# Long-convolution filters on both halves of TensorE's array, with the norm's magnitudes added on GpSimd

## The chip, the cores and the metric

The kernel runs on one core of one Trainium2 chip. The metric is the device time of one execution in microseconds (us), the median of several runs. All line numbers are those of the kernel before the change.

## What is computed

A backbone of two layers over 512 latent tokens and 256 context tokens of width 1024. Each layer has attention, a short convolution and a long ("Hyena") convolution in parallel, and then a mixture of 16384 experts of which 16 are picked for each token and head. The part that the change touches makes the filters of the long convolution:

```python
z = jnp.concatenate([t, jnp.cos(bands * w), -jnp.sin(bands * w)], axis=-1)
h = jnp.sin(f1 * (z @ w1 + b1))
h = jnp.sin(f2 * (h @ w2 + b2))                      # (L, 64)
h = (h @ w3).reshape(L, HY_ORDER, 2, HY_W)           # 2 orders, 2 directions, 512 channels
h = h * jnp.exp(-t[:, :, None] * jnp.abs(decay))[:, :, None, :]
h = h / jnp.sum(jnp.abs(h), axis=(0, 2), keepdims=True)
hf, hb = h[:, :, 0], h[:, :, 1]
k = jnp.concatenate([hf, jnp.zeros_like(hf[:1]), hb[:0:-1]], axis=0)
return jnp.fft.rfft(k, axis=0)
```

L is 512 for the latents (both layers) and 256 for the context (first layer alone). The sum of magnitudes runs over all L times and both directions, for each order and channel.

## The kernel before

The program is a row of phases with a barrier between them. In a phase each engine has a list of instructions of its own, in the order in which the code issues them, and they meet at semaphores. Nothing is planned at run time: what stands behind a wait on an engine's list waits too.

**Hidden rows.** `FilterMlp` (L689) makes the 64 hidden rows of the filter's network. TensorE multiplies (L717), VectorE adds the bias and scales (L726), GpSimd reduces the angle in nine steps (L741 to L754) and ScalarE takes the sine (L760); then the same again for the second layer of the network. In layer 1 this runs inside `phase_mod`, which streams 24 blocks of modulation weights: ScalarE rounds block n (L827), VectorE makes its low part (`split`, L264), TensorE multiplies (L872), and a row copy `keep` (L821) follows every second block. The first sine stands behind block 12, the second behind block 23 and ahead of the last `keep`; the filter's matmuls on TensorE stand behind blocks 2 and 13, VectorE's part behind 3 and 14. VectorE ends the stage with six normalisations (L910) and the modulation step (L912, L917), TensorE turns it (L884), ScalarE copies it out (L845) and SyncE stores it (L800). In layer 2 the same lies in `phase_mod_beside`, beside the expert gathers.

**Filters, layer 1.** `phase_spectrum` (L1898) runs four times: latents order 0 and 1, context order 0 and 1, each ahead of its long convolution. For each tile t of 128 times (nt = 4 for latents, 2 for the context) TensorE multiplies the 64 hidden rows by the two direction blocks of w3 (L1941), in the upper 64 rows of the array, VectorE multiplies by the window (L1983; the window is ScalarE's exponential, L1970), ScalarE takes the absolute value (L1975), and TensorE sums it over the times by a matmul with ones, two per tile, accumulated in bank 4 (L1931, `norm`). Then VectorE folds the two directions (L1996, L1998), tile 0 last, after a row that needs the norm (L1991). TensorE's spectrum jobs (L1960), nine of four tiles for latents and five of two for the context, take the tiles in the order 1, 2, ..., 0 and use the cosine and sine tables.

**Filters, layer 2.** `phase_spectrum_beside` (L2025) runs twice and does the same while the last experts of layer 1 are worked off: gathers by GpSimd (L490), dots by VectorE (L650), weights by ScalarE (L503, L507, L514), sums by TensorE (L535). `Share` gives each engine a part of these after each tile or job; 50 gathers fall on the 13 steps of one such phase. GpSimd issues gathers up to three past a step's share (`FETCH`) into a ring of 8 buffers, and a gather waits until TensorE has used the buffer. The norm matmuls there are L2073, the filter's L2081, absolute value L2120, window multiply L2150, folds L2137 to L2143, jobs L2102. `filter_weights` (L2018) lists the loads of the next filter's weights.

The two f32 passes of a matmul are two instructions in the profile.

Of the kernel before, what the change touches and what calls it, by code (L numbers as in the profile page):

```python
# [27 lines left out]
P = 128  # L28
# [11 lines left out]
W_BR = 512  # L40
# [648 lines left out]
class FilterMlp:  # L689
# [67 lines left out]
    def scalar(self, act, i, hidden):  # L757
        act.wait_ge(self.reduced, i + 1)
        out = hidden if i else self.h1
        self.c.nc.scalar.activation(out[0:FH, 0:self.width], self.r[0:FH], ACT.Sin).then_inc(self.sined, 1)  # L760


def phase_mod(c, layer, lay):
# [19 lines left out]
    with Phase(nc) as ph:  # L783
# [32 lines left out]
        def _(act):  # L816
# [6 lines left out]
            for n in range(2 * chunks):  # L823
                act.wait_ge(w_landed[n % RAW], 16 * (n // RAW + 1))
                if n >= DEEP:
                    act.wait_ge(halves_done, n - DEEP + 1)
                nc.scalar.activation(hi[n % DEEP], raw[:, n % RAW], ACT.Copy).then_inc(hi_ready, 1)  # L827
                if n >= 3 and n % 2:
                    keep((n - 3) // 2)
                if SQUARES <= n < SQUARES + NT:  # L830
                    t = n - SQUARES
                    if layer == 0 and t == 0:
                        act.wait_ge(x_in, 64)
                    if t >= 2:
                        act.wait_ge(sq, t - 1)
                    nc.scalar.activation(junk[:, t % 2], c.xs[:, t], ACT.Square,
                                         accum_out=c.stat[:, 0, t:t + 1]).then_inc(sq, 1)
                if n == SQUARES + NT + 1:
                    act.wait_ge(ms, 1)
                    nc.scalar.activation(c.stat[:, 1, 0:NT], c.stat[:, 1, 0:NT], ACT.Sqrt).then_inc(root, 1)  # L840
                if n in (12, 23):
                    mlp.scalar(act, n // 23, lay.hidden)
# [3 lines left out]
                                 ACT.Copy).then_inc(rows_made, 1)  # L846

# [7 lines left out]
        def _(pe):  # L855
# [9 lines left out]
            for n in range(2 * chunks):  # L865
# [11 lines left out]
                if n in (2, 13):  # L877
                    mlp.tensor(pe, n // 13)
# [8 lines left out]
        def _(dve):  # L887
# [7 lines left out]
            for n in range(2 * chunks):  # L895
# [4 lines left out]
                if n in (3, 14):  # L900
                    mlp.vector(dve, n // 14)
# [996 lines left out]
def phase_spectrum(c, layer, length, order, lay):  # L1898
# [7 lines left out]
    w3, absdec = c.at(152, 2 * W_BR), c.at(190, W_BR)  # L1906
# [6 lines left out]
    with Phase(nc) as ph:  # L1913
# [3 lines left out]

        @ph.block.sync
        def _(sp):
            sp.dma_start(w3[0:FH, :], io["hy_w3"][layer][:, order * 2 * W_BR:(order + 1) * 2 * W_BR]).then_inc(w3_in, 16)  # L1920
# [6 lines left out]
        def _(pe):  # L1927
            def norm(t):
                pe.wait_ge(ab_d, t + 1)
                for d in range(2):  # L1930
                    last = nc.tensor.matmul(c.bank(4), c.ones[:], ab[t % 2][:, d * W_BR:(d + 1) * W_BR],  # L1931
                                            start=(t == 0 and d == 0), stop=(t == nt - 1 and d == 1))
                last.then_inc(normed, 1)

            c.warm_up(ph, pe, 7)
            pe.wait_ge(w3_in, 16)
            for t in range(nt):
                if t >= 2:
                    pe.wait_ge(hw_d, t - 1)
                for d in range(2):  # L1940
# [22 lines left out]

        @ph.block.scalar
        def _(act):
# [12 lines left out]
        def _(dve):  # L1978
# [7 lines left out]
            for t in t_order:  # L1986
                if t == 0:
                    dve.wait_ge(normed, nt)
# [29 lines left out]
def filter_weights(c, layer, order):  # L2018

    io = c.io  # L2020
    return [(c.at(126, 2 * W_BR)[0:FH, :], io["hy_w3"][layer][:, order * 2 * W_BR:(order + 1) * 2 * W_BR]),
            (c.at(130, W_BR), io["hy_decay"][layer][order:order + 1].to_broadcast([P, W_BR]))]


def phase_spectrum_beside(c, layer, order, lay, share, keep):  # L2025
# [5 lines left out]
    w3, absdec, win, hw = c.at(126, 2 * W_BR), c.at(130, W_BR), c.at(80, nt, W_BR), c.at(136, nt, 2 * W_BR)  # L2031
    ab, rnorm, bias, kre_b = [c.at(at, 2 * W_BR) for at in (189, 193)], c.at(197, W_BR), c.at(199, W_BR), c.at(201, W_BR)
    KEPT = 4
    kept_at = c.at(88, KEPT, W_BR)
# [5 lines left out]
    with Phase(nc, gathers=True) as ph:  # L2040
# [4 lines left out]
        top_stored, copied = ph.sem("top_stored"), ph.sem("lowest_copied")  # L2045

        @ph.block.sync
        def _(sp):
# [16 lines left out]
            if order == 0:  # L2065
                sp.wait_ge(next_in, 32)

        @ph.block.tensor
        def _(pe):
            def norm(t):  # L2070
                pe.wait_ge(ab_d, t + 1)
                for d in range(2):
                    last = nc.tensor.matmul(c.bank(NORM), c.ones[:], ab[t % 2][:, d * W_BR:(d + 1) * W_BR],  # L2073
                                            start=(t == 0 and d == 0), stop=(t == nt - 1 and d == 1))
                last.then_inc(normed, 1)

            for t in range(nt):
                if t >= 1:
                    pe.wait_ge(hw_d, t)
                for d in range(2):  # L2080
                    last = nc.tensor.matmul(c.bank(d), h2[0:FH, t * P:(t + 1) * P], w3[0:FH, d * W_BR:(d + 1) * W_BR],  # L2081
                                            start=True, stop=True)
# [27 lines left out]
        def _(act):  # L2110
# [4 lines left out]
            for t in range(nt):  # L2115
                share.scalar(act, t)
                act.wait_ge(hw_d, t + 1)
                if t >= 2:
                    act.wait_ge(normed, t - 1)
# [5 lines left out]
        def _(pool):  # L2125
            for n in range(nt + len(jobs)):
                share.gpsimd(pool, n)

        @ph.block.vector
        def _(dve):  # L2130
            st = Steps(dve, steps)

            def fold(t):
                if t == 0:
                    dve.wait_ge(normed, nt)
# [672 lines left out]
```

## Time and profile before

| | us |
|---|---|
| median of 3 runs | 5476.33 |
| lowest, highest run | 5467.39, 5478.78 |
| the profiled execution | 5477.74 |
| its span, first to last instruction | 5476.0 |
| TensorE busy | 3768.7 (69%) |
| VectorE busy | 3331.5 (61%) |
| GpSimd busy | 2029.4 (37%) |
| ScalarE busy | 1989.0 (36%) |
| GpSimd's gather queue, share of 16 DMA engines | 60.0% |

PE is TensorE's matmuls, PEld its weight loads, DVE VectorE, ACT ScalarE, POOL GpSimd, SP SyncE. Busy times do not add up to the span, for the engines overlap. A row of the timeline gives start, length, engine, line, the work and, in brackets, how long the engine stood idle before it and what released it. PEclk is TensorE's granted clock, 1.00 being 2.4 GHz and 0.50 being 1.2 GHz.

### The profile page before, as it was taken

The numbers are of one execution on the slowest core, as the hardware profiler recorded it, in microseconds if no ns is written. First come the engines' busy times: TensorE is split into PE (matmuls) and PEld (weight loads), VectorE is DVE, ScalarE is ACT, GpSimd is POOL, SyncE is SP. The second block draws the span as 40 slices with busy tenths as digits, with TensorE's granted clock in tenths as the row PEclk, the third lists the DMA queues.
The fourth block names the chain that finished last, engine by engine and source line by source line (L and its number), as shares of the span: only waits on it lengthen the run. The fifth ranks groups of instructions, "written<-read, shape, count | busy, mean of one in ns | idle before, by whom it ended". The sixth has DMA issues, their size and how long they took to land. (4 is left out here: it accounts for less than half of the span.)

```text
span 5476.0 us, 59697 instructions
## 1 busy us (share of the span) xinstructions
PE 3768.7 (69%) x19520; PEld 1835.7 (34%) x19520; DVE 3331.5 (61%) x7026; ACT 1989.0 (36%) x5136; POOL 2029.4 (37%) x1533
## 2 busy tenths in 40 slices
PE   6899879977555555556567768778976555555554
PEld 3677348866111111111122224455853111111111
DVE  7623351233777777777677777655135777777776
ACT  5422012222433434344354344405223344343343
POOL 5121003222444444444473345401433444444443
PEclk8999889988777777776778889889988777777777
DMA  5011001122999999999999988810327999999998
GB/s 235 16 47 66 4 25 60 64 83 110 421 416 414 410 413 418 411 417 416 372 360 359 357 340 361 330 65 30 97 78 301 420 406 416 414 415 416 411 418 350
DMA packets 230356, 1528.24 MB, mean 279 GB/s; under 512 B 26132, under 2 KB 26708, under 8 KB 58012
## 3 DMA queue, kind: packets, MB, share of 16 engines
q0 software_dynamic: 184320, 1342.26, 60.0%
q1 hardware_dynamic: 45724, 182.16, 9.0%
q8 instruction: 154, 2.52, 0.2%
q14 instruction: 158, 1.29, 0.1%
HBM read 1513.21 MB, written 11.11 MB: 278 GB/s over the span
## 5 line engine op out<-in xcount | busy, mean ns | idle before, releaser
L535 PE MATMUL psum<-arena 64*64 64x512 f32 x10240 | 1775.8, 828 | 1239.6 <-ACT arena L514 1216.0
L490 POOL DMA_INDIRECT arena<-in_uv,arena x1280 | 1456.4, 1138 | 1749.8 <-PE psum L535 1327.7
L650 DVE SCALAR_TENSOR_TENSOR arena<-arena 128x1024 f32<-128x1024 f32 x1280 | 1629.3, 1273 | 731.0 <-DMA arena<-in_uv,arena 685.0
L535 PEld LDWEIGHTS psum<-arena 64*64 64x64 f32 x10240 | 419.0, 170 | 2535.3 <-ACT arena L514 1909.4
L1548 PE MATMUL psum<-view_at,view_at 128*128 128x512 f32 (+1 forms) x4896 | 970.8, 359 | 22.5 <-PEq L164 12.9
L264 POOL TENSOR_TENSOR view_at<-view_at,view_at 128x1024 fp32r<-128x1024 f32 (+1 forms) x192 | 454.3, 2375 | 1354.1 <-ACT view_at L298 1313.2
L503 ACT ACTIVATE arena<-arena 128x1 f32<-128x1 f32 x1280 | 258.1, 202 | 1827.3 <-DVE arena L650 1786.9
L1548 PEld LDWEIGHTS psum<-view_at,view_at 128*128 128x128 f32 x4896 | 816.3, 192 | 198.0 <-issue 67.0
L514 ACT ACTIVATE arena<-arena 128x64 f32<-128x64 f32 x1280 | 445.2, 348 | 52.0 <-PE psum L535 10.2
L507 ACT ACTIVATE arena<-arena 128x1 f32<-128x1 f32 x1280 | 376.9, 294 | 46.6 <-ACT arena L503 0.4
L298 ACT ACTIVATE view_at<-view_at 128x1024 fp32r<-128x1024 f32 (+1 forms) x176 | 164.2, 939 | 328.7 <-DMA view_at<-in_w_in 185.1
L2384 DVE TENSOR_TENSOR view_at<-view_at,psum 128x768 f32<-128x768 f32 (+1 forms) x48 | 39.4, 821 | 376.4 <-PE psum L1548 376.4
L264 DVE TENSOR_TENSOR view_at<-view_at,view_at 128x2048 fp32r<-128x2048 f32 (+5 forms) x106 | 177.4, 1700 | 87.2 <-ACT view_at L2350 36.4
L2447 PE MATMUL psum<-view_at,view_at 128*128 128x512 f32 x480 | 113.9, 400 | 35.2 <-DVE view_at L264 34.0
L2244 ACT ACTIVATE arena<-psum 128x256 f32<-128x256 f32 (+2 forms) x17 | 7.2, 421 | 301.3 <-PE psum L2233 301.3
L1018 PE MATMUL psum<-view_at,cond 128*4 128x512 f32 x192 | 65.0, 467 | 70.2 <-ACT view_at L974 45.4
L2447 PEld LDWEIGHTS psum<-view_at,view_at 128*128 128x128 f32 x480 | 92.9, 194 | 55.9 <-issue 34.6
L503 ACT ACT_TABLE_LOAD x85 | 109.1, 1283 | 2.9 <-PEq L164 1.5
L1268 PE MATMUL psum<-view_at,view_at 128*128 128x256 f32 (+1 forms) x528 | 93.3, 338 | 17.4 <-PEq L164 17.4
L650 DVE DVE_READ_ACCUMULATOR arena<-arena 128x1 f32 x1280 | 104.9, 82 | 0.0
L471 ACT ACT_TABLE_LOAD x80 | 102.6, 1283 | 1.4
L557 DVE MAX8 arena<-arena 128x8 f32<-128x128 f32 (+1 forms) x240 | 81.5, 339 | 35.2 <-DVE arena L555 0.5
(246 smaller groups left out, 3506.0 us busy)
## 6 DMA issues: line engine op xcount, KB each, us to landing
view_at<-in_w_in SPq DMA_DIRECT2D x108, 512.0 KB, 5.5
view_at<-in_w_mod SPq DMA_DIRECT2D x48, 1024.0 KB, 12.9
arena<-in_uv,arena POOLq DMA_INDIRECT x1280
view_at<-in_w_br SPq DMA_DIRECT2D x48, 256.0 KB
view_at<-in_w_out SPq DMA_DIRECT2D x16, 512.0 KB, 9.3
view_at<-in_wq SPq DMA_DIRECT2D x16, 512.0 KB, 3.4
arena<-mod_rows SPq DMA_DIRECT2D x12, 512.0 KB
keep_spectrum<-arena SPq DMA_DIRECT2D x18, 256.0 KB, 2.6
```

The source lines that it names most:

```text
L264: return eng.tensor_tensor(lo, x, hi.bitcast(F32), ALU.subtract)
L298: self._high(act, lambda out, x: self.c.nc.scalar.activation(out, x, ACT.Copy), n)
L471: self.c.nc.scalar.activation(self.exps[:, u % 2], self.topc, ACT.Exp, bias=self.small[:, u % 2, 0:1], accum_out=self.small[:, u % 2, 1:2] ...
L490: nc.gpsimd.indirect_dma_start(out=self.slots[i % self.ring], out_offset=None, in_=self.table, in_offset=bass.IndirectOffsetOnAxis(ap=self ...
L503: nc.scalar.activation(self.gelus[:, q, k:k + 1], self.dots[:, q, k:k + 1], ACT.Gelu).then_inc(self.act_steps, 1)
L507: nc.scalar.activation(self.scaled[:, q, k:k + 1], self.gelus[:, q, k:k + 1], ACT.Copy, scale=self.probs[:, q, k:k + 1]).then_inc(self.act ...
L514: nc.scalar.activation(self.diag[:, i % 4], self.ident2, ACT.Copy, scale=self.scaled[:, q, k:k + 1]).then_inc(self.diag_ready, 1)
L535: last = nc.tensor.matmul(self.c.psum[tokens, at:at + 512], self.diag[rows, k % 4], self.slots[k % self.ring][rows, D + h * 512:D + (h + 1 ...
L650: nc.vector.scalar_tensor_tensor(out=self.junk, in0=self.slots[i % self.ring][:, 0:D], scalar=1.0, in1=self.h2_turned if i % 2 else self.h ...
L1268: last = nc.tensor.matmul(out, h[:, k, at], m[:, lo:hi, k, :], start=(k == 0 and i == 0), stop=(k == KD - 1 and i == 2))
L1548: last = nc.tensor.matmul(c.psum[:, at + lo:at + hi], a[:, k], b[:, k, lo:hi], start=(k == 0 and i == 0), stop=(k == kt - 1 and i == 2))
L2447: last = nc.tensor.matmul(c.bank(2 * (t % 4) + h), a[:, k, t * P:(t + 1) * P], b[:, 4 * h:4 * h + 4, k, :], start=(k == 0 and i == 0), sto ...
```

## The change

The second sine of `FilterMlp` is now written twice, to partitions 0 to 63 and 64 to 127. The two direction blocks of w3 are loaded, by two transfers, one to the upper and one to the lower 64 partitions, so that the two filter matmuls of a tile use different halves of the array. The norm's matmuls, two a tile, are gone: GpSimd adds the absolute values of all tiles and directions into one tile `total` (7 additions for the latents, 3 for the context), and one matmul with ones sums that over its partitions. ScalarE's wait for a free buffer of absolute values is now for GpSimd's additions. In `phase_mod` the first sine moves from behind block 12 to behind block 11, the second to the very end of ScalarE's list, and the second filter matmul and VectorE's part for it move up one block.

```diff
@@ FilterMlp.scalar
         self.c.nc.scalar.activation(out[0:FH, 0:self.width], self.r[0:FH], ACT.Sin).then_inc(self.sined, 1)
+        if i:
+            self.c.nc.scalar.activation(out[FH:P, 0:self.width], self.r[0:FH], ACT.Sin).then_inc(self.sined, 1)
@@ phase_mod, ScalarE
-                if n in (12, 23):
-                    mlp.scalar(act, n // 23, lay.hidden)
+                if n == 11:
+                    mlp.scalar(act, 0, lay.hidden)
             keep(chunks - 1)
             act.wait_ge(mod_turned, 2)
             nc.scalar.activation(turned_rows[0:N_MOD], c.psum[0:N_MOD, 0:2 * P].rearrange("p (s q) -> p s q", s=2),
                                  ACT.Copy).then_inc(rows_made, 1)
+            mlp.scalar(act, 1, lay.hidden)
@@ phase_mod, TensorE and VectorE
-                if n in (2, 13):
-                    mlp.tensor(pe, n // 13)
+                if n in (2, 12):
+                    mlp.tensor(pe, n // 12)
...
-                if n in (3, 14):
-                    mlp.vector(dve, n // 14)
+                if n in (3, 13):
+                    mlp.vector(dve, n // 13)
@@ phase_spectrum (phase_spectrum_beside has the same add_abs)
+        def add_abs(pool, t):
+            pool.wait_ge(ab_d, t + 1)
+            for d in range(2):
+                part = ab[t % 2][:, d * W_BR:(d + 1) * W_BR]
+                if t == d == 0:
+                    continue
+                if t or d > 1:
+                    pool.wait_ge(added, 2 * t + d - 1)
+                first = total if t else ab[0][:, 0:W_BR]
+                nc.gpsimd.tensor_tensor(total, first, part, ALU.add).then_inc(added, 1)
...
-            sp.dma_start(w3[0:FH, :], io["hy_w3"][layer][:, order * 2 * W_BR:(order + 1) * 2 * W_BR]).then_inc(w3_in, 16)
+            for d, rows in enumerate((TOP, BOTTOM)):
+                sp.dma_start(w3[rows], io["hy_w3"][layer][:, (2 * order + d) * W_BR:(2 * order + d + 1) * W_BR]).then_inc(w3_in, 16)
...
-            pe.wait_ge(w3_in, 16)
+            pe.wait_ge(w3_in, 32)
             for t in range(nt):
                 if t >= 2:
                     pe.wait_ge(hw_d, t - 1)
-                for d in range(2):
-                    last = nc.tensor.matmul(c.bank(2 * (t % 2) + d), h2[0:FH, t * P:(t + 1) * P], w3[0:FH, d * W_BR:(d + 1) * W_BR],
+                for d, rows in enumerate((TOP, BOTTOM)):
+                    last = nc.tensor.matmul(c.bank(2 * (t % 2) + d), h2[rows, t * P:(t + 1) * P], w3[rows],
                                             start=True, stop=True)
                 last.then_inc(made, 1)
-                if t >= 1:
-                    norm(t - 1)
-            norm(nt - 1)
+            pe.wait_ge(added, 2 * nt - 1)
+            nc.tensor.matmul(c.bank(4), c.ones[:], total, start=True, stop=True).then_inc(normed, 1)
...
+        @ph.block.gpsimd
+        def _(pool):
+            for t in range(nt):
+                add_abs(pool, t)
...
-                    act.wait_ge(normed, t - 1)
+                    act.wait_ge(added, 2 * t - 3)
...
-                    dve.wait_ge(normed, nt)
+                    dve.wait_ge(normed, 1)
@@ phase_spectrum_beside
-                share.tensor(pe, t, 0, 2)
-                if t >= 1:
-                    norm(t - 1)
                 share.tensor(pe, t)
-            norm(nt - 1)
+            pe.wait_ge(added, 2 * nt - 1)
+            nc.tensor.matmul(c.bank(NORM), c.ones[:], total, start=True, stop=True).then_inc(normed, 1)
...
             for n in range(nt + len(jobs)):
                 share.gpsimd(pool, n)
+                if n < nt:
+                    add_abs(pool, n)
```

The filter matmuls, the loads (`filter_weights`) and the two waits for the norm change in `phase_spectrum_beside` as in `phase_spectrum`.

## Rows read from the trace of the kernel before

**Rows 1.** Stretches: length, busy us (count) of PE, PEld, DVE, ACT, POOL; PEclk; DMA share; GB/s.

```profile
2200.00:2400.00 200.00, 114.09 (x636) 27.07 (x640) 150.79 (x368) 80.97 (x257) 90.66 (x81) 0.73 1.01 412
...
2893.00:2945.00 52.00, 39.16 (x162) 11.90 (x162) 35.64 (x66) 20.06 (x57) 18.03 (x16) 0.81 0.93 364
```

**Rows 2.** Timeline, first latent filter: start us, length us, engine, line, work, idle before.

```profile
519.35 0.58 SPq L1921 DMA_DIRECT2D arena<-in_hy_decay  x1
...
522.44 4.02 PE L1941 MATMUL psum<-arena 64*128 64x512 f32 x8 [0.25 <-DMA arena<-in_hy_w]
...
525.48 2.36 DVE L1983 TENSOR_TENSOR arena<-psum,arena 128x1024 f32<-128x1024 f32 x2 [7.36 <-ACT arena L1970]
...
543.26 25.16 PE L1960 MATMUL psum<-arena 128*128 128x512 f32 x58 [0.37 <-DVE arena L1998]
```

**Rows 3.** Timeline, the three other filters of layer 1.

```profile
620.29 7.16 PE L1941 MATMUL psum<-arena 64*128 64x512 f32 x8
...
644.86 20.44 PE L1960 MATMUL psum<-arena 128*128 128x512 f32 x47 [0.38 <-DVE arena L1998]
...
727.39 1.22 DVE L1983 TENSOR_TENSOR arena<-psum,arena 128x1024 f32<-128x1024 f32 x1 [0.74 <-PE psum L1941]
...
735.48 4.99 PE L1960 MATMUL psum<-arena 128*128 128x512 f32 x11 [1.37 <-DVE arena L1998]
...
778.75 1.23 DVE L1983 TENSOR_TENSOR arena<-psum,arena 128x1024 f32<-128x1024 f32 x1 [2.19 <-PE psum L1941]
...
786.50 6.28 PE L1960 MATMUL psum<-arena 128*128 128x512 f32 x14 [1.37 <-DVE arena L1998]
```

**Rows 4.** GpSimd's element-wise work: groups by shape, then the extremes of one line (ns).

```profile
L264 POOL TENSOR_TENSOR view_at<-view_at,view_at 128x512 fp32r<-128x512 f32 x48 | 67.4, 1404 | 17.9 <-ACT view_at L298 17.9
...
L741 POOL TENSOR_SCALAR arena<-arena 64x768 f32<-64x768 f32 x2 | 16.6, 8308 | 30.8 <-DVE arena L726 30.8
...
L741 POOL TENSOR_SCALAR arena<-arena 64x512 f32<-64x512 f32 x2 | 2.1, 1063 | 5.8 <-DVE arena L726 5.8
...
L264 POOL TENSOR_TENSOR view_at<-view_at,view_at x192: 1277/2394/5603, 106.0 to 4123.8; 128x1024 fp32r<-128x1024 f32 x132, 128x512 fp32r<-128x512 f32 x48, 128x2048 fp32r<-128x2048 f32 x12
```

**Rows 5.** VectorE's folds of the first latent filter, grouped by line.

```profile
L1998 DVE SCALAR_TENSOR_TENSOR arena<-arena 128x512 f32<-128x512 f32 x4 | 2.8, 691 | 0.1
```

**Rows 6.** TensorE's clock after a wait: a stretch, then two runs of matmuls.

```profile
598.00:602.00 4.00, 4.00 (x7) 1.66 (x6) 0.00 (x0) 0.00 (x0) 0.00 (x0) 0.54 0.00 0
...
596.14 16.72 PE L2233 MATMUL psum<-arena 128*128 128x512 f32 x32 [5.64 <-DVE arena L2264]
...
210.04 1.56 PE L1431 MATMUL psum<-arena 64*128 64x512 f32 x8 [1.35 <-ACT arena L1512]
```

**Rows 7.** Timeline, the first modulation stage around its two sines.

```profile
53.40 0.84 ACT L760 ACTIVATE arena<-arena 64x768 f32<-64x768 f32 x1 [2.40 <-POOL arena L754]
...
86.34 1.28 ACT L760 ACT_TABLE_LOAD   x1
...
93.72 0.84 ACT L760 ACTIVATE arena<-arena 64x768 f32<-64x768 f32 x1 [6.10 <-POOL arena L754]
...
98.27 0.38 ACT L845 ACTIVATE arena<-psum 48x256 f32<-48x256 f32 x1 [3.22 <-PE psum L884]
...
88.41 7.15 DVE L910 TENSOR_SCALAR arena<-arena,stat 128x1024 f32<-128x1024 f32 x6
...
97.00 0.26 DVE L912 TENSOR_TENSOR mod<-psum,cols 128x96 f32<-128x96 f32 x1 [1.43 <-PE psum L860]
```

**Rows 8.** First filter beside the gathers (timeline), then two groups of the page.

```profile
2934.16 1.06 ACT L2120 ACTIVATE arena<-arena 128x1024 f32<-128x1024 f32 x1 [4.32 <-DVE arena L2150]
...
2939.09 0.68 DVE L2137 TENSOR_TENSOR arena<-psum,arena 1x512 f32<-1x512 f32 x1 [2.31 <-PE psum L2073]
...
L490 POOL DMA_INDIRECT arena<-in_uv,arena x1280 | 1456.4, 1138 | 1749.8 <-PE psum L535 1327.7
...
L650 DVE SCALAR_TENSOR_TENSOR arena<-arena 128x1024 f32<-128x1024 f32 x1280 | 1629.3, 1273 | 731.0 <-DMA arena<-in_uv,arena 685.0
```

More of the change, by code:

```diff
@@ L1905, in phase_spectrum @@
     h2 = lay.hidden[:, times]
-    w3, absdec = c.at(152, 2 * W_BR), c.at(190, W_BR)
+    w3, absdec, total = c.at(152, W_BR), c.at(190, W_BR), c.at(200, W_BR)
     win = c.at(156, nt, W_BR)
@@ L1927, in _ @@
         def _(pe):
-            def norm(t):
-                pe.wait_ge(ab_d, t + 1)
-                for d in range(2):
-                    last = nc.tensor.matmul(c.bank(4), c.ones[:], ab[t % 2][:, d * W_BR:(d + 1) * W_BR],
-                                            start=(t == 0 and d == 0), stop=(t == nt - 1 and d == 1))
-                last.then_inc(normed, 1)
             c.warm_up(ph, pe, 7)
-            pe.wait_ge(w3_in, 16)
+            pe.wait_ge(w3_in, 32)
             for t in range(nt):
@@ L2020, in filter_weights @@
     io = c.io
-    return [(c.at(126, 2 * W_BR)[0:FH, :], io["hy_w3"][layer][:, order * 2 * W_BR:(order + 1) * 2 * W_BR]),
-            (c.at(130, W_BR), io["hy_decay"][layer][order:order + 1].to_broadcast([P, W_BR]))]
+    w3, source = c.at(126, W_BR), io["hy_w3"][layer]
+    return [(w3[rows], source[:, (2 * order + d) * W_BR:(2 * order + d + 1) * W_BR]) for d, rows in enumerate((TOP, BOTTOM))] + [
+        (c.at(130, W_BR), io["hy_decay"][layer][order:order + 1].to_broadcast([P, W_BR]))]
 def phase_spectrum_beside(c, layer, order, lay, share, keep):
@@ L2045, in phase_spectrum_beside, with add_abs @@
         top_stored, copied = ph.sem("top_stored"), ph.sem("lowest_copied")
+        added = ph.sem("abs_added")
+        def add_abs(pool, t):
+            pool.wait_ge(ab_d, t + 1)
+            for d in range(2):
+                part = ab[t % 2][:, d * W_BR:(d + 1) * W_BR]
+                if t == d == 0:
+                    continue
+                if t or d > 1:
+                    pool.wait_ge(added, 2 * t + d - 1)
+                first = total if t else ab[0][:, 0:W_BR]
+                nc.gpsimd.tensor_tensor(total, first, part, ALU.add).then_inc(added, 1)
         @ph.block.sync
@@ L2065, in _ @@
             if order == 0:
-                sp.wait_ge(next_in, 32)
+                sp.wait_ge(next_in, 48)
         @ph.block.tensor
         def _(pe):
[L2070 to L2075, printed above, removed]
             for t in range(nt):
@@ L2079, in _ @@
                     pe.wait_ge(hw_d, t)
-                for d in range(2):
-                    last = nc.tensor.matmul(c.bank(d), h2[0:FH, t * P:(t + 1) * P], w3[0:FH, d * W_BR:(d + 1) * W_BR],
-                                            start=True, stop=True)
+                for d, rows in enumerate((TOP, BOTTOM)):
+                    last = nc.tensor.matmul(c.bank(d), h2[rows, t * P:(t + 1) * P], w3[rows], start=True, stop=True)
                 last.then_inc(made, 1)
-                share.tensor(pe, t, 0, 2)
-                if t >= 1:
-                    norm(t - 1)
                 share.tensor(pe, t)
-            norm(nt - 1)
+            pe.wait_ge(added, 2 * nt - 1)
+            nc.tensor.matmul(c.bank(NORM), c.ones[:], total, start=True, stop=True).then_inc(normed, 1)
             if order == 0:
@@ L2118, in _ @@
                 if t >= 2:
-                    act.wait_ge(normed, t - 1)
+                    act.wait_ge(added, 2 * t - 3)
                 nc.scalar.activation(ab[t % 2], hw[:, t], ACT.Abs).then_inc(ab_d, 1)
@@ L2134, in fold @@
                 if t == 0:
-                    dve.wait_ge(normed, nt)
+                    dve.wait_ge(normed, 1)
                     dve.wait_ge(bias_in, 16)
```

6 lines of the change are left out of this document (3 added, 3 removed).

## Prediction

> **What bounds the kernel now.** I read the stretch rows first. In the long gather stretches the DMA engines are full: share 1.01 at 412 GB/s [rows 1]. One gather brings 128 rows of 8 KB, 1.05 MB, so it takes 1.05 MB / 412 GB/s = 2.55 us, and GpSimd, which issues it, waits for TensorE to give a buffer back (1327.7 us in all), as VectorE waits for landings (685.0 us) [rows 8]. The two filters of layer 2 lie inside such a stretch, at a DMA share of 0.93 [rows 1]: what they cost is what they take from the gathers. The four filters of layer 1 have no cover at all. There the timeline is a chain of TensorE, VectorE and ScalarE, tile by tile, and it ends where the last tile of the first spectrum job is multiplied; from there TensorE runs without a gap at 25.16 / 58 = 0.43 us an instruction, two instructions for a matmul [rows 2]. So each filter of layer 1 is worth what moves that one start: 543.26, 644.86, 735.48 and 786.50 us [rows 2, 3].
>
> **Price list.** A matmul is 0.87 us at the 2.4 GHz level and 7.16 / 8 x 2 = 1.79 us at 1.2 GHz [rows 2, 3]. Two matmuls in different halves overlap: the attention scores, two of 512 columns and two of 256, take 1.56 us [rows 6] where one after the other would take 2 x 0.87 + 2 x 0.43 = 2.6. A pair of 512 is thus about 1.04 us, or 2.1 at the lower level. A multiply by the window is 1.23 us, an absolute value 1.06, a fold 0.69 a step (two steps a tile) [rows 2, 5, 8].
> An addition on GpSimd, 128x512, has no row of its own. The nearest is the split of the same shape: mean 1.40 us, and the least of its line 1.28 [rows 4]. Between two of them I put 0.1 us for the semaphore. The 7 additions of a latent filter then take at least 7 x 1.38 = 9.7 us, the 3 of a context filter 4.1.
> On top comes VectorE. The same GpSimd operation of the filter's angles took 8.31 us beside a row of VectorE splits and 1.06 us (two thirds of the elements) where VectorE was seldom in its way [rows 4]. So a fold can cost the additions its whole 0.69: 6 x 0.69 = 4.1 us at most for a latent filter, 1.4 for a context one. I take half, 2.1 and 0.7, since the folds cannot all meet an addition.
> The Trainium skill (SBUF — State Buffer, "Who interferes with whom") says that a VectorE instruction with two SBUF inputs and a GpSimd one that reads SBUF exclude each other for a whole instruction. Taken strictly that is my upper bound, and it speaks against moving work from TensorE to GpSimd; the 8.31 us agrees with it.
> The clock: after a wait of 5.64 us TensorE's granted clock was 0.54, near its 1.2 GHz level, and 32 instructions took 16.72 us instead of 32 x 0.43 = 13.9 [rows 6]. That is 2.8 us lost. Before the change TensorE had norm matmuls all through the filter; after it, it waits some 8 to 11 us for the last addition, so I charge these 2.8 us.
>
> **Layer 1, first latent filter.** Removed: 8 norm matmuls, of which 1 comes back; the filter pairs take half. Added: 7 additions and one more transfer, whose issue pushes the decay's behind it by about 0.53 us. The first multiply was released by the windows [rows 2] and so moves from 525.48 to 526.0; then 528.4 ends the second. The pair for tile 2 starts at 527.2 and the four multiplies are done at 530.9, some 6 us sooner than now. Nothing of that reaches the end, because the additions are next: the first one can start when the first absolute value is done, 528.8, and the last ends at 538.4 (nothing in its way) to 542.6; I take 540.5. Behind it stand one norm matmul and three tiles of the first job: 4 x 0.87 + 2.8 = 6.3 us, which also covers the last fold. Last tile at 546.9 instead of 543.26: **+3.6** (+1.5 to +5.7; without the clock loss 2.8 less).
> **Second latent filter.** Its first matmuls ran at 1.2 GHz from 620.29 (8 instructions in 7.16 us) and tile 2 waited behind the norm [rows 3], so there is more to gain. Pair at 622.7, windows' exponentials done at 624.9, first absolute value 626.0, additions over at 635.7 to 639.8, middle 637.8; plus 6.4 gives 644.2 against 644.86: **-0.7** (-2.8 to +1.3).
> **Context filters.** Three additions. First one: second multiply now at 727.39 [rows 3]; after, 727.2 to 728.4, additions done 732.4 to 733.8, middle 733.1; then 0.1, the norm matmul cold 1.8 and the three small steps of fold 0, 2.2: 737.2 against 735.48, +1.7. Second: multiply now at 778.75, after at 776.0; additions over at 781.9; 786.0 against 786.50, -0.5. Here the first tile of job 0 lies beside fold 0, and of the clock's 2.8 us about 1.0 is still to come in each: **+2.7 and +0.5** (each -1.5 to +1.5 around it).
> The sum of the four is **+6.1**.
>
> **First modulation stage.** The first sine waited for GpSimd until 53.40 us [rows 7], with split 12 already done by ScalarE ahead of it. Now split 12 stands behind the sine; ScalarE is nearly gapless from there, so its splits and VectorE's low parts come up to 1.9 us later, and VectorE's six normalisations end at 88.41 + 7.15 + 1.9 = 97.5 instead of 95.6 [rows 7]. The second sine (93.72) no longer holds the last row copy, but the modulation step starts at 97.5 against 97.00: nothing is won. GpSimd's angles start as before, since TensorE's second filter matmul waits for split 12 too. At the end ScalarE's copy, 98.27 us, shifts to 98.8; behind it now come a table load (1.28) and two sines of 0.84, to about 102.0. Before, the two stores behind that copy closed the stage near 100.2. **+1.8** (0 to +3.5). In the second modulation stage a sine more, about 0.65 us, lies beside ScalarE's waits: 0.
>
> **Layer 2, two filters beside the gathers.** Here GpSimd is the issuer. It has issued three gathers past the tile's share when it comes to the additions, and then waits until VectorE's dots of the share, the multiply and the absolute value are done; behind it stand all further gathers. From the landing: dot 1.23 + multiply 1.23 + absolute 1.06 + two additions 2.8 to 4.2 + issue 0.94 to 1.14 = 7.3 to 9.7 us [rows 8], against 3 x 2.55 = 7.65 us of DMA work in flight. So a tile costs between nothing and 2.0 us. The first tiles of both filters fall into waits that are there anyway; six at 0.5 are +3. At the end of the filter the fold of tile 0 follows the last absolute value (2934.16) by 4.9 us (2939.09) [rows 8]; after, 1.06 + 2.8 + 0.7 + 1.8 = 6.4, so +1.5 twice, +3. Against it: TensorE loses a norm of 4 instructions and half a filter pair per tile, and buffers come back earlier; -2 per filter. **+2** (-6 to +16).
>
> **Sum.** 6.1 + 1.8 + 2 = +9.9 us. The profiled execution took 5477.74 us (span 5476.0), 1.4 above the median of the runs, 5476.33. So 5476.33 + 9.9 = 5486.2; I say **5486 us**. A measurement of this kernel can tell about 0.2%, 11 us, from no change: 5465.4 to 5487.3 is "the same".
>
> **Rivals.**
> (a) *GpSimd's wait drains the gathers.* Place: each filter tile of layer 2, where the additions and VectorE's 1.23 us dots get in each other's way. It decides once the hold is longer than 7.65 us in every tile. For it: dots read two SBUF operands, and the DMA share of 0.93 leaves little to catch up with. Against: the DMA queue already sits out waits of GpSimd today. 8 x 2.0 = +16 in place of +2: 5476.33 + 23.9 = 5500. Chance 0.20, slower.
> (b) *Additions hide, clock stays up.* Additions at 1.38, no collisions, no 2.8 us: -1.3, -5.6, +0.1, -2.1 for layer 1's filters; modulation +0.5; layer 2 -4. Sum -12.4: 5464. Against: the 5.64 us wait shows what even a shorter one does. Chance 0.17, of which 0.12 is faster.
> (c) *TensorE's relief shows in the gathers.* The forecast, but layer 2 gives -6: 5478, the same. For it: GpSimd's largest wait is the one for TensorE. Chance 0.17.
> (d) *The halves do not overlap.* Then a pair stays at 1.7 us; it is off the chain behind the additions except for the first tile, under +1 a filter, and lies in the forecast's own range.
> The forecast has 0.46: from 5478 to 5494, a little more than half of it below 5487.3 (0.26 the same, 0.20 slower). Together: faster 0.12, same 0.48, slower 0.40. The range reaches to (b) on one side and through (a) on the other: 5466 to 5503.
>
> **What would show it.** Right: in layer 1's filters the multiplies end 5 us sooner, seven rows of about 1.4 us on GpSimd follow each other, TensorE has one gap of 8 us or more before a single norm matmul, its clock is near 0.5 behind it, and spectrum jobs start at about +4, -1, +2 and 0 us relative to the stage's start. Wrong: additions of 1.0 us, or of over 2; a clock of 1.0 after the gap; a modulation stage that is not longer. In layer 2 the proof is GpSimd's wait for ScalarE's absolute value and the DMA share of the filter stretches: if it stays at 0.93 or rises, (a) is wrong.

## The result and the profile after

The changed kernel took 5487.44 us in the median of 11 runs (5481.01 to 5494.82), against 5474.8 us for the kernel before (11 runs, 5467.39 to 5480.89): ratio 1.0026, 95% interval 1.0018 to 1.0034, or 12.6 us slower. Six more runs of it, set against 22 of the kernel before, gave 1.0032 [1.0020, 1.0044]. The forecast was 5486 us (+9.9), range 5466 to 5503.

The page of the changed kernel's profile: the span, the engines, and the new group of additions in layer 1 (mean 1457 ns). It answers to the table of before.

```profile
span 5489.3 us, 59617 instructions
...
PE 3713.4 (68%) x19452; PEld 1814.6 (33%) x19452; DVE 3354.0 (61%) x7026; ACT 1990.1 (36%) x5138; POOL 2087.4 (38%) x1567
...
L1932 POOL TENSOR_TENSOR arena<-arena 128x512 f32<-128x512 f32 x20 | 29.1, 1457 | 241.6 <-ACT arena L1989 239.8
```

TensorE lost 55 us of work, GpSimd and VectorE gained 58 and 22.5: for VectorE, which does nothing new, that is the first hint. The timeline of the first latent filter after answers to [rows 2]. In its lines L1951 is the pairs, L1997 the window multiply, L1932 the additions, L2010 and L2012 the folds, L1955 the one norm matmul, L1969 the spectrum jobs.

```profile
530.03 3.25 PE L1951 MATMUL psum<-arena 64*128 64x512 f32 x8 [0.15 <-DMA arena<-in_hy_w]
...
536.84 10.71 POOL L1932 TENSOR_TENSOR arena<-arena 128x512 f32<-128x512 f32 x7 [14.45 <-ACT arena L1989]
...
538.62 1.23 DVE L1997 TENSOR_TENSOR arena<-psum,arena 128x1024 f32<-128x1024 f32 x1 [0.52 <-PE psum L1951]
...
541.45 1.64 DVE L2012 SCALAR_TENSOR_TENSOR arena<-arena 128x512 f32<-128x512 f32 x1
...
547.60 2.08 PE L1955 MATMUL psum<-arena,ones 128*128 128x512 f32 x2 [9.03 <-POOL arena L1932]
...
549.47 10.98 PE L1969 MATMUL psum<-arena 128*128 128x512 f32 x21
```

The chain is the forecast one: the last multiply starts 12.1 us after the stage's warm-up at 526.55 instead of 17.1 (535.96 after 518.86 before), then seven additions in 10.71 us, and TensorE stands still for 9.03 us and goes on cold: two norm instructions in 2.08 us. The clock in the gap and behind it, and both filters of layer 2, in the stretches after (columns as in [rows 1]):

```profile
538.60:547.60 9.00, 0.00 (x1) 0.01 (x1) 8.91 (x6) 1.72 (x2) 8.42 (x6) 0.50 0.25 106
547.60:554.00 6.40, 6.40 (x9) 2.82 (x10) 5.40 (x6) 0.00 (x0) 0.00 (x0) 0.57 0.00 0
2896.60:2953.90 57.30, 28.32 (x140) 7.90 (x144) 41.96 (x77) 25.65 (x63) 30.25 (x24) 0.69 0.87 332
3053.00:3109.80 56.80, 30.36 (x136) 8.50 (x140) 38.78 (x74) 25.43 (x63) 29.57 (x24) 0.68 0.75 289
```

The same two filters before, each cut from ScalarE's first window instruction to VectorE's reciprocal:

```profile
2887.50:2941.10 53.60, 39.87 (x154) 12.19 (x158) 36.60 (x76) 25.51 (x63) 19.69 (x17) 0.77 0.94 368
3040.00:3090.10 50.10, 41.64 (x158) 12.54 (x162) 35.53 (x75) 25.37 (x63) 19.36 (x17) 0.74 0.86 325
```

They grew from 103.7 to 114.1 us, and the DMA share fell from 0.94 to 0.87 and from 0.86 to 0.75. The gathers of layer 1's experts go on for another 440 us behind the filters, and by TensorE's last expert sum (L535) 3.7 of these 10.4 us had been taken back: from the first filter's start to there it was 646.4 us before and 653.1 after (+6.7).

**Where the time went, by stages.** "Filters" is the sum of layer 1's four filter stages, warm-up to warm-up. "Layer 2" is the stretch just described, from its first filter's start to the last expert sum beside it. Each number is one profiled execution, and the repeats show what one is worth.

| Kernel | first modulation stage ends | filters, layer 1 | layer 2 | ratio to before |
|---|---|---|---|---|
| before | 101.6 | 168.4 | 646.4 | 1 |
| before, new modulation order only | 103.8 | 171.5 | 640.7 | 1.0005 |
| changed | 106.4 | 174.6 | 653.1 | 1.0026 |
| changed, again | 106.0 | 171.7 | 648.1 | 1.0032 |
| changed, modulation order back | 105.8 | 174.5 | 653.7 | 1.0028 |
| changed, only the late sine | 101.0 | 174.1 | 653.1 | one run, 1.0015 |

Averaged over the kernels that share a part's code, the filters of layer 1 cost +4.2 us (170.0 for two, 174.1 for six: the four above and two kernels of experiments 2 and 3 below, 175.6 and 174.2). Layer 2 cost +8.5 (643.5 for two, 652.0 for four; two later kernels with the same layer 2, in experiments 4 and 5, had 653.9 and 653.1). Executions of the same code lie up to 4 us apart in the first and 6 in the second, so each of these means is good to some 2 to 4 us.

### The profile page after: what moved, and what is told of

The parts are those of the page before. It is cut to its first block and busy times, and to the rows that moved or that the text cites. A ratio compares the mean times of both kernels' runs of the same rounds, so it can differ in the third digit from the quotient of the medians.

```text
span 5489.3 us, 59617 instructions
## 1 busy us (share of the span) xinstructions
PE 3713.4 (68%) x19452; PEld 1814.6 (33%) x19452; DVE 3354.0 (61%) x7026; ACT 1990.1 (36%) x5138; POOL 2087.4 (38%) x1567
## 5 line engine op out<-in xcount | busy, mean ns | idle before, releaser
L535 PE MATMUL psum<-arena 64*64 64x512 f32 x10240 | 1764.7, 823 | 1241.6 <-ACT arena L514 1221.4
L490 POOL DMA_INDIRECT arena<-in_uv,arena x1280 | 1465.8, 1145 | 1689.7 <-PE psum L535 1279.7
L650 DVE SCALAR_TENSOR_TENSOR arena<-arena 128x1024 f32<-128x1024 f32 x1280 | 1638.6, 1280 | 724.3 <-DMA arena<-in_uv,arena 687.9
L535 PEld LDWEIGHTS psum<-arena 64*64 64x64 f32 x10240 | 416.8, 169 | 2537.3 <-ACT arena L514 1916.8
L1551 PE MATMUL psum<-view_at,view_at 128*128 128x512 f32 (+1 forms) x4896 | 968.0, 359 | 20.8 <-PEq L164 12.1
L1932 POOL TENSOR_TENSOR arena<-arena 128x512 f32<-128x512 f32 x20 | 29.1, 1457 | 241.6 <-ACT arena L1989 239.8
L650 DVE DVE_READ_ACCUMULATOR arena<-arena 128x1 f32 x1280 | 104.7, 82 | 0.0
```

The costliest lines, as they stand in the source:

```text
L490: nc.gpsimd.indirect_dma_start(out=self.slots[i % self.ring], out_offset=None, in_=self.table, in_offset=bass.IndirectOffsetOnAxis(ap=self ...
L535: last = nc.tensor.matmul(self.c.psum[tokens, at:at + 512], self.diag[rows, k % 4], self.slots[k % self.ring][rows, D + h * 512:D + (h + 1 ...
L650: nc.vector.scalar_tensor_tensor(out=self.junk, in0=self.slots[i % self.ring][:, 0:D], scalar=1.0, in1=self.h2_turned if i % 2 else self.h ...
L1551: last = nc.tensor.matmul(c.psum[:, at + lo:at + hi], a[:, k], b[:, k, lo:hi], start=(k == 0 and i == 0), stop=(k == kt - 1 and i == 2))
```

## The experiments

**1. The modulation stage.** First, the changed kernel with ScalarE's, TensorE's and VectorE's places in `phase_mod` as before:

```diff
-                if n == 11:
-                    mlp.scalar(act, 0, lay.hidden)
+                if n in (12, 23):
+                    mlp.scalar(act, n // 23, lay.hidden)
...
-            mlp.scalar(act, 1, lay.hidden)
```

> The changed kernel with the first modulation stage's order as before (sines behind blocks 12 and 23, filter matmul behind 13, VectorE's part behind 14); everything else as changed. Theory: the parts add up, and this one is worth what the traces show at its end: the first instruction of the next stage on TensorE at 106.4 us in the changed kernel against 101.6 before. So it starts at 101.6 to 102.4 (the second copy of the second sine, 0.75 us, stays) and the time is 5487.4 - 4.5 = 5483, still 8 us above before. Rival: what is late there is caught up later, or was the run's own; then the next stage starts early and the time stays at 5487.

1.0028 [1.0016, 1.0041]: nothing came back, and the stage ended at 105.8 us though its order was the old one. Then only the second sine last, with the first at 12 and TensorE and VectorE at 13 and 14:

> The changed kernel with the first sine behind block 12, the second filter matmul behind 13 and VectorE's part behind 14 as before; only the second sine stays last on ScalarE. Theory (the block that moved behind the first sine costs, the late sine does not): next stage on TensorE at 101 to 102.5 us instead of 106.4. Rival (late sine costs most): 104 or more.

101.0 us; the time of this single run was 5480.56 us, which is too little to tell. The two kernels of experiment 6, which have this order too, ended the stage at 103.8 and 101.0. Last, the kernel before with the new order and nothing else:

> The kernel before with nothing changed but the first modulation stage's order: first sine behind block 11, second last, second filter matmul behind 12, VectorE's part behind 13. Theory: worth +1.8 us, as forecast (ScalarE one block later, a table load and a sine behind the last copy), time ratio 1.0003, not to be told from 1. Rival (the 4.9 us of the first trace are the order's): ratio 1.0009, next stage at 105 to 106.5.

1.0005 [0.9996, 1.0014]. So with the old order (both sines) three executions ended the stage at 101.6, 102.7 and 105.8 us, with the whole new one eight at 103.6 to 106.4 (means 103.3 and 104.9). With only the second sine late, three had a mean of 102.0: no trace speaks against the late sine, and if anything costs, it is the part that moved up one block. No run has that part alone. The new order's tail is real, in the timeline of the changed kernel:

```profile
102.19 0.38 ACT L847 ACTIVATE arena<-psum 48x256 f32<-48x256 f32 x1 [3.62 <-PE psum L887]
102.58 1.28 ACT L760 ACT_TABLE_LOAD   x1
103.88 0.84 ACT L760 ACTIVATE arena<-arena 64x768 f32<-64x768 f32 x1
104.75 0.84 ACT L762 ACTIVATE arena<-arena 64x768 f32<-64x768 f32 x1
...
106.43 5.54 PE L1147 MATMUL psum<-ident,arena 128*128 128x128 f32 x36 [4.28 <-PEq L164]
```

The copy at 102.19 stood at 98.27 before [rows 7]; behind it come a table load and two sines that were not there. But the stage itself differs by 4 us from one execution to the next, so the part is worth some 0 to 3 us (+1.6 by the means), and the two profiles compared alone (+4.8) overstate it.

**2. Taking GpSimd's additions back.** The pairs stay. The norm goes back to TensorE, first in layer 2 only, then in layer 1 too (there with the modulation order of before as well):

```diff
-            pe.wait_ge(added, 2 * nt - 1)
-            nc.tensor.matmul(c.bank(NORM), c.ones[:], total, start=True, stop=True).then_inc(normed, 1)
+                if t >= 1:
+                    norm(t - 1)
+            norm(nt - 1)
...
-                if n < nt:
-                    add_abs(pool, n)
```

> The changed kernel, but in layer 2's two filters the norm is summed on TensorE again (two matmuls with ones per tile), GpSimd only issues gathers; the two halves stay. Theory (GpSimd's wait and additions hold back the gathers): the first filter phase of layer 2, from its first ScalarE instruction to that of the second, goes from 156.4 us back to 152.5 or a little less, and the second gains 4 to 6 us as well; the time is 5487.4 - 4 = 5483 or somewhat below. Rival (the gather stretch absorbs it: what a filter phase loses, the waits behind it give back): the phases get shorter, the end of the gather stretch does not move, 5487. Second rival (run to run spread of the gathers): the phases stay at 156.

1.0003 [0.9994, 1.0012].

> Only the two halves are left of the change: norm on TensorE in all six filters, modulation order as before. Theory (additions, clock and order make the loss; the pair of halves alone gains): layer 1's four filter stages, measured from warm-up to the next stage's warm-up, go below the 54.7, 58.3, 26.3 and 29.1 us of before by about 0.9 us for each tile whose matmul stood in the chain: -1.8, -4, -0.5, -1.5, together -8; layer 2 unchanged or -2. Time 5474.8 - 8 = 5467. Rival (the pair is off the chain, VectorE and ScalarE set it): stages as before, 5475. Rival (halves do not overlap here, one after the other): filter pair of four instructions stays 1.7 us at full clock.

0.9982 [0.9973, 0.9991]: the pairs alone are a gain of 9.1 us on the medians (5456.6 against 5465.66). The expectation had put 4 us on layer 2's additions; they cost 1.0026 or 1.0032 less 1.0003, some 13 to 16 us by the ratios, and 12 by the traces (652.0, the mean of four, to 640.0, the mean of the four kernels with the pairs alone in layer 2: 637.6, 640.1, 639.7 and 642.6). Layer 1's filters fall from 175.6 to 163.9 us with the second step. The stretches of the first of the two kernels in layer 2's filters:

```profile
2893.50:2943.50 50.00, 35.60 (x154) 10.36 (x158) 36.76 (x77) 25.66 (x63) 18.53 (x17) 0.75 0.99 399
3043.00:3091.50 48.50, 32.21 (x158) 9.64 (x162) 35.47 (x75) 25.34 (x63) 16.97 (x17) 0.84 0.90 365
```

These 98.5 us are the lowest of the four kernels with this code (100.2 in the second kernel here, 102.0 and 101.2 in the two of experiment 6; 103.7 and 102.5 with the code of before), and their DMA share in the first filter is 0.96 to 0.99 against 0.94 and 0.95: the gathers do go faster once TensorE has less to do and GpSimd nothing more. So both forces that the forecast set against each other in layer 2 are there: about -3.5 (643.5 to 640.0) and +12 in size.

**3. How the additions hurt the gathers.** GpSimd's timeline and VectorE's in the first filter of layer 2, changed kernel (L2073 an addition, L490 the issue of a gather, L650 a dot):

```profile
2912.69 0.93 POOL L490 DMA_INDIRECT arena<-in_uv,arena  x1 [0.30 <-issue]
...
2919.53 4.08 POOL L2073 TENSOR_TENSOR arena<-arena 128x512 f32<-128x512 f32 x2 [5.90 <-ACT arena L2138]
...
2923.76 0.95 POOL L490 DMA_INDIRECT arena<-in_uv,arena  x1
...
2929.52 1.23 DVE L650 SCALAR_TENSOR_TENSOR arena<-arena 128x1024 f32<-128x1024 f32 x1 [4.03 <-DMA arena<-in_uv,arena]
```

GpSimd issued no gather from 2912.69 to 2923.76, 11.07 us, of which 5.90 was the wait for the absolute value and 4.08 the two additions. Three gathers in flight, the forecast's estimate of the cover, are 7.65 us of DMA work, and VectorE then stood 4.03 us before data. The view of waits in this stretch (2896 to 3110; us in total, times, longest) has eight such waits, and GpSimd's main wait of before is nearly halved. The changed kernel:

```profile
POOL arena L490 <- PE psum L535: 44.3, 21, 5.9
...
POOL arena L2073 <- ACT arena L2138: 38.8, 8, 6.0
```

And the kernel before, 2887 to 3091:

```profile
POOL arena L490 <- PE psum L535: 84.6, 26, 12.1
```

GpSimd used to wait for a buffer with transfers still in flight; now half of its waiting is for a value, while transfers that could start are not issued. The length of a gap alone does not tell the two apart, for the kernel before waited 12.1 us at its longest. To test this, the additions of a tile were put behind the next tile's gathers:

```diff
-                if n < nt:
+                if 1 <= n < nt:
+                    add_abs(pool, n - 1)
+                if n == nt - 1:
                     add_abs(pool, n)
```

> The changed kernel, but in layer 2 GpSimd issues the next tile's gathers before it comes to a tile's additions (the last tile's stay where they are). Theory a (what holds the gathers back is that GpSimd waits for ScalarE's absolute value with gathers queued behind it): the first filter phase of layer 2 goes from 156.4 to about 153, and the time falls by 2 to 4 us. Theory b (it is the additions' own 1.3 to 1.6 us and their meeting with VectorE's dots, or TensorE's wait for the last addition): nothing changes, 156 and 5487.

1.0012 [1.0003, 1.0021]; layer 2 took 643.5 us, with the same additions as in the changed kernel (652.0 in the mean). The time fell by 8 to 11 us by the ratios, more than either theory had. Its two stretches:

```profile
2891.10:2943.30 52.20, 26.95 (x136) 7.50 (x140) 41.07 (x77) 25.54 (x63) 29.81 (x24) 0.73 0.92 365
3043.20:3095.60 52.40, 27.51 (x136) 7.65 (x140) 40.43 (x75) 25.41 (x63) 29.38 (x24) 0.70 0.83 315
```

104.6 against 114.1 us (110.5 to 114.1 in the six kernels with the changed layer 2), and POOL as busy as in the changed kernel (29.81 and 29.38 against 30.25 and 29.57). Most of the cost was the place, not the work: the held gathers, not the additions' own microseconds. What is left over the pairs alone (98.5 to 102.0) lies in the main at the filters' ends, which this edit leaves as they were: from the last absolute value to fold 0 TensorE and VectorE wait for the last additions, 6.25 us instead of 4.93 in the first filter, and 6.2 instead of 3.1 in the second (4.6 in the profile of the new modulation order).

**4. TensorE's clock in layer 1.** Small matmuls (32 for latents, 24 for the context, 128 columns, into an unused bank; their result is used by nothing) fill TensorE's gap ahead of the norm matmul:

```diff
+            for _ in range(32 if nt == NT_LAT else 24):
+                nc.tensor.matmul(c.psum[:, 7 * 512:7 * 512 + P], c.ident[:], c.ones[:], start=True, stop=True)
             pe.wait_ge(added, 2 * nt - 1)
```

> The changed kernel with small matmuls (identity by ones, 128 columns, to a spare bank) in TensorE's gap before the norm matmul of layer 1's filters: 32 for latents, 24 for the context. They compute nothing that is used. Theory (2 to 3 us of every filter of layer 1 is the clock that falls in the gap): the norm matmul's two instructions take 0.9 us instead of 2.1, the clock is 1.0 behind it, the four stages go from 57.5, 56.8, 30.9, 29.4 to 54.7, 54.2, 28.5, 27.2, the time falls by about 9 us. Rival (the small matmuls do not keep the clock, or the additions' own length sets the stage): stages stay within 1 us.

1.0008 [0.9999, 1.0017]; the four stages fell to 164.5 us. The timeline of the first filter:

```profile
534.09 7.41 PE L1955 MATMUL psum<-ones,ident 128*128 128x128 f32 x64
...
542.85 1.13 PE L1957 MATMUL psum<-arena,ones 128*128 128x512 f32 x2 [1.35 <-POOL arena L1932]
```

And the stretch from 0.85 us ahead of the norm matmul:

```profile
542.00:549.00 7.00, 6.15 (x15) 2.80 (x16) 6.90 (x6) 0.00 (x0) 0.80 (x1) 1.00 0.01 2
```

The clock is 1.00 instead of 0.57 and the norm matmul takes 1.13 us instead of 2.08. The additions were as long as ever (10.73 us), so it was the clock that this saved: 9.6 us against the mean of the six kernels with the changed filters, 2.4 a filter.

**5. The lock between VectorE and GpSimd.** In layer 1 the folds wait for all additions:

```diff
+                    dve.wait_ge(added, 2 * nt - 1)
```

> The changed kernel, but in layer 1 VectorE's folds wait until all additions of GpSimd are done, so that they never meet. Theory (the additions are long because folds are in their way): an addition takes 1.26 us, seven take 7 x 1.34 = 9.4 us instead of 10.7 to 11.0, and the folds take 0.69 each instead of 1.64; the stages get longer all the same, since the folds now stand behind (+1 to +3 us each). Rival (an addition is 1.5 us by itself): seven take 10.7 as now.

A single run, 5479.68 us. The additions by line (nanoseconds: least, median, most) in the changed kernel:

```profile
L1932 POOL TENSOR_TENSOR arena<-arena x20: 1261/1524/1592, 536.8 to 791.5; 128x512 f32<-128x512 f32 x20
```

And in this one:

```profile
L1932 POOL TENSOR_TENSOR arena<-arena x20: 1259/1262/1274, 533.2 to 786.5; 128x512 f32<-128x512 f32 x20
```

In its first filter:

```profile
533.18 9.52 POOL L1932 TENSOR_TENSOR arena<-arena 128x512 f32<-128x512 f32 x7 [14.71 <-ACT arena L1989]
...
543.53 0.69 DVE L2013 SCALAR_TENSOR_TENSOR arena<-arena 128x512 f32<-128x512 f32 x1
```

An addition with nothing in its way is 1.26 us, with folds 1.52; seven of them took 9.52 us in place of 10.71. A fold is 0.69 us alone and 1.64 beside them (541.45 above). The expectation that the stages would get longer was wrong: they were 171.3 us, no longer than those of the changed filters (171.7 to 175.6), because the late folds ran beside the cold norm matmul and the cold first job, which cover them. Whether they got shorter one profile can't tell.

**6. What is left without GpSimd.** The pairs alone with the second sine last:

> As the run with only the two halves left, plus the second sine of the first modulation stage last on ScalarE, the first sine still behind block 12. Theory (it was moving the first sine one block up that cost 4.9 us, not the late second one): the last row copy no longer waits for GpSimd, the modulation step comes at 95.7 instead of 97.0, but a table load and two sines close the stage: next stage at 101 to 102, time equal to the run without it within 1 us. Rival (the late sine is the cost): next stage at 103.5 or later, 2 to 3 us more.

0.9977 [0.9968, 0.9986], not to be told from 0.9982. Then in layer 1 all pairs first and the norm matmuls behind them, so that tile 2 never waits behind a norm:

```diff
-                if t >= 1:
-                    norm(t - 1)
-            norm(nt - 1)
+            for t in range(nt):
+                norm(t)
```

> Both halves, norm on TensorE in all six filters, second sine late; and in layer 1 TensorE multiplies all tiles of a filter first and sums the norms behind them. Theory (in layer 1 the chain runs through the pairs of tiles 2 and 3, which stand behind the norms of tiles 0 and 1): multiplies end some 4 us sooner in a latent filter, the four norms then take 4 x 1.74 us in a row at full clock and set the end: latent stages 55.9 and 52.7 go to 53 and 50, context ones (two tiles, nothing stands in between) stay at 27.7 and 25.6. Time 4 to 6 us under the version without it, about 0.9969 of before. Rival (TensorE's clock or ScalarE's absolute values set it): stages stay.

0.9964 [0.9950, 0.9977], 5453.74 against 5473.01 us: the lowest of all versions, 19 us below the kernel before, though its interval overlaps that of 0.9977. Its four stages add up to 156.2 us, against 163.9 and 161.9 in the two kernels with the pairs alone and 168.4 and 171.5 with the filters of before, and TensorE goes from the norm into the jobs without a gap:

```profile
532.72 8.21 PE L1935 MATMUL psum<-arena,ones 128*128 128x512 f32 x16
...
540.76 11.75 PE L1963 MATMUL psum<-arena 128*128 128x512 f32 x27
```

**7. The changed kernel again, and mended.** The changed kernel unaltered, and then with all three remedies (small matmuls, late folds, gathers first):

> The changed kernel once more, beside the others of this call, for the spread of the first modulation stage and for a time that the next three can be set against. Theory (that stage's length differs from execution to execution: 101.6 before, 105.8 with the order of before, 103.6 to 106.4 with the changed one): the next stage starts anywhere from 102 to 106.5 us. Layer 1's four filter stages together 174.6 within 1, the two filter parts of layer 2 (to the reciprocal) 57 and 56; ratio to before 1.0026 within 0.001.

1.0032 [1.0020, 1.0044].

> The changed kernel with its three costs mended and the additions left on GpSimd: small matmuls that keep the clock in layer 1's gap, folds of layer 1 behind the additions, and in layer 2 the next tile's gathers ahead of a tile's additions. Theory (the three are separate and add up): layer 1's stages 174.6 - 10 - 1 = 163, layer 2's filter parts 52 each, time 5487.4 x (1 - 0.0036) or about 0.999 of before: the change's GpSimd part can be made harmless, not better than TensorE's norm (0.998). Rival (mending one uncovers the next): ratio stays above 1.0005.

1.0008 [0.9999, 1.0017], 5478.37 us: 9.3 below the changed kernel in the same comparison, yet no faster than the small matmuls alone. The remedies don't add up, and the timeline of its first filter shows why in layer 1:

```profile
542.80 0.69 DVE L2013 TENSOR_TENSOR arena<-arena 128x512 f32<-128x512 f32 x1 [7.08 <-POOL arena L1932]
...
546.93 1.12 PE L1971 MATMUL psum<-arena 128*128 128x512 f32 x2 [0.20 <-DVE arena L2015]
...
548.97 25.16 PE L1971 MATMUL psum<-arena 128*128 128x512 f32 x58 [0.92 <-DVE arena L2015]
```

With the clock kept up, the first job no longer covers the late folds, and TensorE waits for them (0.20 and 0.92 us): 170.8 us for the four stages against 164.5 with the small matmuls alone. In layer 2 its filters took 107.2 us (changed: 114.1 and 111.2), and the layer 648.0 us against 653.9 with the small matmuls alone. So the two profiles set -5.9 us in layer 2 against +6.3 in layer 1, which fits the equal ratios. In experiment 3 the same edit had given 643.5 in layer 2. By the ratios that edit was worth 1.4 to 2.0 in a thousand (1.0012 against 1.0026 and 1.0032), 8 to 11 us, and the intervals of 1.0012 and 1.0026 overlap a little.

## Why the prediction was right

**Layer 1's filters, +6.1 forecast: +4.2 measured.** The two profiles side by side give 174.6 - 168.4 = +6.2, with +2.8, -1.5, +4.6 and +0.3 against the forecast +3.6, -0.7, +2.7 and +0.5; that near agreement is partly luck, as the repeats show. The terms held one by one. Additions: 1.38 a step was taken from [rows 4], 9.52 / 7 = 1.36 measured. The lock: half of 6 x 0.69 = 2.1 us was taken for the additions, 10.71 - 9.52 = 1.2 measured. The Trainium skill (SBUF — State Buffer, "Who interferes with whom") has a VectorE instruction with two SBUF inputs and a GpSimd one that reads SBUF shut each other out for a whole instruction. The trace agrees in part: one side does lose a good instruction's time, but it is VectorE, 0.95 us a fold (1.64 for 0.69), while GpSimd loses 0.26 an addition. The forecast's upper bound, every fold's whole 0.69 us lost by GpSimd, was 4.1 us, over three times the measured loss. The clock: 2.8 us charged for each latent filter and 1.9 for each context one (the cold norm matmul 0.9 and 1.0 behind it), 9.4 in all; 9.6 measured.

**The pair, 1.04 us from [rows 6].** The kernel with the pairs alone has one between norm matmuls that took 1.13 us at full clock:

```profile
539.66 1.13 PE L1944 MATMUL psum<-arena 64*128 64x512 f32 x4
```

Rival (d), halves that do not overlap, would have had 1.74: it is out. Why the pairs alone are faster, and with the norms behind them faster still, the forecast had not asked; the expectation of experiment 6 did, and its latent stages of 53 and 50 us came out at 53.7 and 49.2.

**Modulation, +1.8.** 1.0005 [0.9996, 1.0014] for it alone, +3 us within -2 to +8, and +1.6 by the means of the traces: nothing speaks against the size, and nothing here can measure it.

**Layer 2, +2 forecast: +8.5 measured. This is the term that was mis-sized.** The step that failed reads "So a tile costs between nothing and 2.0 us. The first tiles of both filters fall into waits that are there anyway; six at 0.5 are +3". Of the three terms there, the filters' ends came as forecast: +1.5 twice had been put, and the first grew by 1.3 us, the second by 1.7 to 3.1. The relief of TensorE, taken at -4, was -3.5 in the kernels where GpSimd had nothing more to do. The holds are what is left of the additions' 12 us: some 9 in place of 3. From the last gather issued ahead of a tile's additions to the first behind them, the eight tiles of the changed kernel's profile took 7.6 to 11.1 us, 9.0 in the mean: a mean wait of 4.9 for the absolute value, and additions of 1.6 us, up to 4.08 for two. Held against the forecast's cover of 7.65 us, what sticks out adds up to 10.6 us there and to 5.9 in the second profile of the same kernel. So the idea of a hold set against the transfers in flight was right, and the 0.5 was not: it took a value near the lower end of a range in which a short hold gives nothing back for a long one. The range itself was added up wrongly, for its upper terms (1.23 + 1.23 + 1.06 + 4.2 + 1.14) make 8.9 us and not 9.7, so that a tile's most would have been 1.2 us and not 2.0; the measured holds go beyond either.

**The rivals.** (a), gathers drained by GpSimd's wait, is what happened in layer 2, less completely than it said: it put +16 for the layer, where the additions cost +12, the pairs gave 3.5 back and +8.5 was left. The DMA share fell, as it said. But not every hold was longer than 7.65 us, two of the eight being 7.6, and the time did not reach 5500. (b), additions hidden and the clock up, is out: gap 9.03 us, clock 0.57. (c) is true of the pairs without the additions (a DMA share of up to 0.99 at 399 GB/s), not of the change.

**The sum.** 4.2 + 8.5 + 0 to 3 is 13 to 16 us, and 12.6 and 14.7 were measured. The two profiles alone add up to 6.2 + 4.8 + 6.7 = 17.7, while the spans differ by 13.3; the rest, -4.4, lies in stages that the change doesn't touch. The forecast of +9.9 was 2.7 us low, with layer 2 some six short and layer 1 two high: that the total came so close is in part luck, for the two errors have opposite signs.

## What to carry to other kernels

An engine that issues gathers should not wait for a computed value between two issues: put such work behind the next gathers, and hold each wait, the longest above all, against the transfers in flight. Moving work from a busy TensorE to an idle GpSimd helps a stage like layer 1's filters only if the chain gets shorter; here 20 additions opened gaps in which TensorE fell to its lower clock. And try the parts of an edit apart: the whole was 12.6 us slower, the pairs alone 9 us faster.

## What was not expected of the hardware

**VectorE bears the lock.** Beside GpSimd's additions a fold grew by 0.95 us and an addition by 0.26.

**TensorE's clock at a stage's start varies with the same code.** In the kernel before, the first eight filter instructions took 4.02 us [rows 2]. In the kernel with the new modulation order alone, whose filter code is the same, the timeline has

```profile
525.21 7.16 PE L1942 MATMUL psum<-arena 64*128 64x512 f32 x8 [0.46 <-DMA arena<-in_hy_w]
```

and that stage took 58.1 us instead of 54.7. The granted clock over these eight instructions was 0.50 there and 0.91 in the kernel before. A single profile of this kernel can't size a filter to better than 3 us.

**Small matmuls hold the clock.** 64 instructions of 128 columns, 7.41 us in all, kept it at 1.00 over a gap that otherwise ended at 0.50; the last 1.35 us of the gap stayed empty without harm.
